# Moving VectorE's wait for its masked copy behind each level's operands, the queries' rotary work behind the fourth level, and the first branch unit ahead of the last gate part

## The reference

```python
hq, hf, hi, hz, aq, ak, av, az, ga, gb = split(rmsnorm(h) @ w_in)
f = lb + (1 - lb) * sigmoid(hf); kA = 1 - f
oA = hgrn2_chunked(hq, log(f), kA, hi)        # S_t = diag(f_t) S_{t-1} + k_t^T v_t
oB = softmax(q1 k1^T) v - lam * softmax(q2 k2^T) v   # q, k with rotary on the first quarter of dims
yA = (rmsnorm(oA) * silu(hz)) @ w_branch_a
yB = (rmsnorm(oB) * silu(az)) @ w_branch_b
h = h + (sigmoid(ga) * yA + sigmoid(gb) * yB) @ w_out
out = rmsnorm(h, final_g)
```

## Time and profile before

| | |
|---|---|
| median of 3 runs | 718.7 us (718.34 to 718.92) |
| profiled execution | 718.66 us, span 716.5 us |
| busy share of the span | PE 97%, DVE 76%, ACT 62%, POOL 23% |
| granted TensorE clock, share of full speed | 0.998 |
| first matmul of head 3 and of head 4 (L845) | 223.38 and 282.39 us |
| chain that ended last | PE 85%, DVE 8%, issue 4% |

### The profile page before, as it was taken

How to read it: one execution, slowest core, us unless ns; L and a number is a source line. 1 busy time by engine, 2 the same in 40 slices (tenths; PEclk the granted TensorE clock), 3 DMA queues, 4 the chain that set the end, 5 groups by cost and what they waited for, 6 DMA issues and landing times.

```text
span 716.5 us, 15635 instructions
## 1 busy us (share of the span) xinstructions
PE 693.7 (97%) x5121; PEld 650.2 (91%) x5121; DVE 542.2 (76%) x1233; ACT 446.6 (62%) x1004; POOL 167.9 (23%) x193
## 2 busy tenths in 40 slices
PE   3999999999999999999999999999999999999996
PEld 2998998999999999999999999999999988888885
DVE  5899869978978978997997897898677662735342
ACT  5553775885796596688588569658776661223232
POOL 2011332233333333233332333323411000000000
PEclk9999999999999999999999999999999999999999
DMA  8357667877867877786877787787777452235103
GB/s 328 126 116 174 147 147 170 174 195 171 179 149 185 191 163 163 165 202 157 176 164 181 175 180 162 165 180 189 165 203 212 143 177 88 98 108 206 59 1 118
DMA packets 51657, 115.58 MB, mean 161 GB/s; under 512 B 5762, under 2 KB 6164, under 8 KB 51620
## 3 DMA queue, kind: packets, MB, share of 16 engines
q0 software_dynamic: 22896, 42.48, 35.1%
q1 hardware_dynamic: 27972, 71.44, 29.3%
q10 hardware_dynamic: 752, 1.18, 0.5%
HBM read 70.51 MB, written 2.10 MB: 101 GB/s over the span
## 4 chain that ended last, share of the span: by engine, by line
PE 85%; DVE 8%; issue 4%; DMA 1%; ACT 1%; DVEq 0%; POOL 0%; SPq 0%; POOLq 0%; ACTq 0%
PE ps L681 23%; PE ps L682 22%; PE ps L683 22%; PE ps L938 3%; PE ps L863 3%; PE ps L966 2%; DVE aa L1884 2%; PE ps L845 1%; DVE w_lo L398 1%; PE ps L955 1%; PE ps L967 1%; PE ps L899 1%; PE ps L898 1%; PE ps L879 1%; PE ps L908 1%
## 5 line engine op out<-in xcount | busy, mean ns | idle before, releaser
L390 ACT ACTIVATE w_hi<-w_raw 128x512 fp32r<-128x512 f32 x216 | 131.9, 622 | 88.6 <-PE ps L683 37.3
L681 PE MATMUL ps<-t_hi,w_hi 128*128 128x256 f32 x576 | 170.2, 296 | 2.3 <-DVE vT_a L1776 1.7
L683 PE MATMUL ps<-t_hi,w_lo 128*128 128x256 f32 x576 | 162.6, 282 | 0.0
L682 PE MATMUL ps<-t_lo,w_hi 128*128 128x256 f32 x576 | 162.6, 282 | 0.0
L681 PE MATMUL ps<-uT_hi,w_hi 128*128 128x272 f32 (+3 forms) x536 | 162.1, 302 | 0.0
L682 PE MATMUL ps<-uT_lo,w_hi 128*128 128x272 f32 (+3 forms) x536 | 155.6, 290 | 0.0
L683 PE MATMUL ps<-uT_hi,w_lo 128*128 128x272 f32 (+3 forms) x536 | 155.3, 290 | 0.0
L617 POOL DMA_DIRECT2D w_lo<-w_raw x84 | 77.6, 924 | 190.2 <-ACT w_lo L392 179.7
L681 PEld LDWEIGHTS ps<-t_hi,w_hi 128*128 128x128 f32 x576 | 109.5, 190 | 7.6 <-issue 6.1
L682 PEld LDWEIGHTS ps<-t_lo,w_hi 128*128 128x128 f32 x576 | 109.8, 191 | 0.0
L683 PEld LDWEIGHTS ps<-t_hi,w_lo 128*128 128x128 f32 x576 | 109.6, 190 | 0.0
(11 more groups left out here) (254 smaller groups left out, 1468.7 us busy)
## 6 DMA issues: line engine op xcount, KB each, us to landing
w_raw<-in_w_in SPq DMA_DIRECT2D x44, 512.0 KB, 4.8
w_lo<-w_raw POOLq DMA_DIRECT2D x84, 256.0 KB, 4.3
w_raw<-in_w_in SPq DMA_DIRECT2D x72, 256.0 KB, 4.4
w_sum<-in_w_in SPq DMA_DIRECT2D x36, 256.0 KB, 3.1
w_raw<-w_raw POOLq DMA_DIRECT2D x36, 256.0 KB, 3.7
w_sum<-w_raw POOLq DMA_DIRECT2D x36, 256.0 KB, 4.5
w_raw<-in_w_branch_a SPq DMA_DIRECT2D x8, 512.0 KB, 3.3
w_raw<-in_w_branch_b SPq DMA_DIRECT2D x8, 512.0 KB, 3.3
```

The lines of the kernel that those rows point to most:

```text
L390: act.activation(part_at(w_hi, j), part_src(pr, j), ACT.Copy).then_inc(pair_hi[j], 1)
L681: pe.matmul(dst, w[0], rhs[0], start=start, stop=False, skip_group_check=True)
L682: pe.matmul(dst, w[0], rhs[1], start=False, stop=False, skip_group_check=True)
L683: return pe.matmul(dst, w[1], rhs[0], start=False, stop=stop, skip_group_check=True)
```

## The change

Four things. In `next_level`, VectorE's wait on `lvl_taken` goes from ahead of the multiplies to ahead of the short product. In `steady`, `rotated_lo(0)`, the queries' shuffle, products and sum go to later places, and `part_lo(p_1_, 1)`, `take_level(3)` and `sum_4` to others. On TensorE levels 4 and 8 come one slot earlier (12 to 11 and 15 to 14) and scores s0 and s1 one later (26 to 27); on ScalarE `rotated_hi(h, 1)` goes ahead of `tanh_z`. At the end of the gates, branch unit 0 goes ahead of the last pair's part 4, on ScalarE and VectorE its split goes ahead accordingly, and the counts of `w_used` follow.

```diff
-B0 = UNITS_END + PARTS * ALL_PAIRS + PART_ORDER.index(4) + 1
+B0 = UNITS_END + PARTS * ALL_PAIRS + 1
-HG_AT = dict(zip(HG_STEPS, (2, 7, 12, 15, 18, 22, 25, 28, 30, 33, 35, 52)))
-AT_AT = dict(zip(AT_STEPS, (26, 26, 28, 33, 33, 35, 35, 37, 37, 39, 42, 46, 48, 55)))
+HG_AT = dict(zip(HG_STEPS, (2, 7, 11, 14, 18, 22, 25, 28, 30, 33, 35, 52)))
+AT_AT = dict(zip(AT_STEPS, (27, 27, 28, 33, 33, 35, 35, 37, 37, 39, 42, 46, 48, 55)))
...
-                return PART_ORDER.index(4) if isinstance(pr.q, int) and (pr.q, j) == (ALL_PAIRS - 1, 4) else 0
+                return 0
...
-            for half in range(2):
-                part(gate_pair(GATES - 1), 4, half, False)
...
                 last.then_inc(w_used, 2)
+                if u == 0:
+                    for half in range(2):
+                        part(gate_pair(GATES - 1), 4, half, False)
...
                 save_p50(p_1_)
+                rotated_hi(h, 1)
                 tanh_z(h, 0)
-                rotated_hi(h, 1)
                 part_hi(act, p_2, 1)
...
-                    free = B0 if u == 3 else UNITS_END + PARTS * (ALL_PAIRS - 1) + min(2 * SLOT_OF[u] + 2, PARTS)
+                    free = B0 + 2 if u == 3 else UNITS_END + PARTS * (ALL_PAIRS - 1) + min(2 * SLOT_OF[u] + 2, PARTS)
...
+                if not more:
+                    branch_hi(0)
                 gate_rest(n + 1, before)
                 gate_11(n + 2, pr)
...
-                    for u in range(3):
+                    for u in (1, 2):
                         branch_hi(u)
...
                     if m > 1:
                         dve.wait_ge(lvl_ready, 7 * h + LEVELS.index(m))
-                        if taken != 0:
-                            dve.wait_ge(lvl_taken, 7 * h + LEVELS.index(m))
                     dve.wait_ge(hg_done, hg(h, f"l{m}"))
...
+                    if m > 1 and taken != 0:
+                        dve.wait_ge(lvl_taken, 7 * h + LEVELS.index(m))
                     mark(dve.tensor_tensor(t_of[2 * m], tk[:, :, 0], tk[:, :, 1], ALU.mult))
...
                     next_level(2, 0)
-                    part_lo(dve, p_1_, 0, 1)
+                    part_lo(dve, p_1_, 0)
                     take_level(1)
                     dve.wait_ge(lvl_taken, 7 * h + 1)
-                    rotated_lo(0)
+                    part_lo(dve, p_1_, 1)
                     take_level(2)
                     q_given()
                     next_level(4)
                     sum_2(dve, p_1_)
                     c_12(0)
-                    swap_pairs(qT[:, :])
+                    take_level(3)
                     c_22(0)
-                    take_level(3)
                     part_lo(dve, p_1_, 5)
                     next_level(8)
+                    swap_pairs(qT[:, :])
+                    sum_4(dve, p_1_)
                     turn_pairs(qT[:, :], META)
-                    sum_4(dve, p_1_)
                     take_level(4)
                     next_level(16)
+                    add_pairs(qT[:, :]).then_inc(rotated, 1)
                     part_lo(dve, p_1_, 6)
-                    add_pairs(qT[:, :]).then_inc(rotated, 1)
                     take_level(5)
                     next_level(32)
+                    rotated_lo(0)
                     part_lo(dve, p_2, 0)
...
+                if not more:
+                    branch_lo(0)
                 c12(pr, gates_at(n + 2)[0][:, HALF:])
...
-            for u in range(UNIT_SLOTS):
+            for u in range(1, UNIT_SLOTS):
                 branch_lo(u)
```

## The result

The changed kernel takes 708.3 us (median of 4 runs, 707.37 to 708.35), the one before 718.5 beside it: a ratio of 0.9855 [0.9838, 0.9872], 10.2 us less. The forecast was 8.6 less. So the kernel gained 1.6 more than forecast.

A forecast was written before the change was run, and what follows sets the result against it. TensorE's time was the bound, with VectorE's 18.34 us chain ending last in each head. Seven heads at 1.13 plus 0.69 in the tail gave 8.60 off 718.66: 710.1 us, with 708.3 to 714.0 to hold 8 in 10.

The forecast's parts named there:

- What bounds the kernel: Whole loop: TensorE's time bounds it, about 57.6 us of work a head, with VectorE's 18.34 us chain ending last.
- The moved wait: VectorE's multiplies behind the masked copies of levels 4, 16, 32, 64 start earlier, saving 1.18 us a head.
- The rotary work: Queries' rotary operations on VectorE only change places; two chained waits swap, adding 0.05 us, so the chain becomes 17.21.
- What TensorE finds: Level groups find operands ready; key transposes go from 248.72 to 247.59, so each head is 1.13 us shorter.
- The thinnest margin: TensorE's level-32 group: level 16's copy ends at 240.66, TensorE asks at about 240.93, a margin of 0.27 us.
- The likeliest case's own range: Total time if the forecast case holds: 708.5 (TensorE's 1.3 a head plus the tail) to 711.8 us.
- Head 1: First steady head in the loop: the same chain as the others and hence the same gain, 1.13 us.
- The tail: Last gate part: branch unit 0 fills TensorE's 0.89 us gap while it waits for VectorE's difference; gain 0.69 us.
- rival (d): In the tail, the branch unit is not ready and TensorE gains nothing there: 710.8 us, chance 0.05.
- Rival (a): VectorE starts the multiply no earlier because it empties itself between operations anyway; only the tail wins: 718.0 us, chance 0.06.
- Rival (b): In the heads, a thin margin or late DMA returns 2 to 5 us: 712 to 715 us, chance 0.14.
- Rival (c): The transfer behind `sum_4(p_1)` ends last; 6.1 us to landing removes the heads' gain, 7 us gives 723.6; chance 0.05.

The follow-up runs named there:

- shorter chain: Changed kernel with the low half of part 1 of the third pair moved from ahead of the last masked copy to behind it: 708.05 us, ratio 0.9845.
- old slots: Changed kernel with TensorE's earlier places restored (levels 4 and 8 one slot later, scores 0 and 1 one earlier): 710.54 us, ratio 0.9884.
- both: Changed kernel with part 1's low half behind the last masked copy and, before the loop, ScalarE's third-part high half ahead of the second norm: 707.87, 707.27, 707.98 us.

## Why the prediction was right and where it was wrong

**What bounds the kernel: right.** TensorE's time, with VectorE's chain ending last at the transposes. Taking the chain down took the heads down, and once the chain was short enough nothing more was to be had ("shorter chain"). Of the wait of 0.1 to 0.3 us that I had forecast at the transposes 0.04 is left.

**The moved wait: right in kind, too small in size. This is where the sum failed.** The failed step reads: "For the longer copy (0.73) I take its length less the 0.09 by which operations overlap here (0.71 long, next one 0.62 later: 232.08 to 232.70), so 0.64." It is 0.52, in the changed kernel and in the one with the wait alone. Level 4 therefore saves 0.41, not 0.29; levels 16, 32 and 64 save 0.29 to 0.30 as said. The chain is 0.24 shorter than my 17.21, and the head gained 0.24 more than my 1.13: 0.12 of it is this term, 0.09 the next one, and 0.03 is spread over several rows. I took the overlap from a plain operation, while the trace of before had the very thing in head 0, an independent operation behind a masked copy of this length, 0.55 from start to start. Its VectorE timeline:

```profile
50.32 0.74 DVE L1884 COPY_PREDICATED aa<-masks,ps 128x256 f32<-128x256 uint8 x1
...
50.87 0.84 DVE L1914 STREAM_SHUFFLE e<-qT 128x512 f32<-128x512 f32 x1
```

**The rotary work: nearly right.** The sum counted its places at +0.05. It missed that what now stands behind level 1's copy is a weight's low half (L398, 0.78 behind the copy) and no longer the keys' (L1930, 0.87), 0.09 less. With 0.12 and 0.09 the chain would have been 17.21 - 0.21 = 17.00; it is 16.97. Both stand behind a wait of the same kind as the moved ones, `dve.wait_ge(lvl_taken, 7 * h + 1)` directly behind `take_level(1)`, which the change left where it was. Why one of the two starts 0.09 sooner than the other behind the same copy and the same wait stays open.

**What TensorE finds: right to a few hundredths.** With 2.33 taken off, I had the groups of levels 8, 16 and 32 at 231.91, 235.26 and 238.60; they stand at 231.92, 235.28 and 238.63. The thinnest margin, 0.27 at level 32, is 0.50 (the copy into sq ends at 238.13), again those two hundred nanoseconds. Only the transposes are off, 245.02 for 245.26, since their time came from the chain. The bound I set, "TensorE alone would allow about 1.3", was 1.41 (59.02 - 57.61), the low end of my own 247.3 to 247.45, which allows 1.27 to 1.42. So the head gained 1.37 where I had 1.13, and seven heads 9.3 where I had 7.9: 1.4 of the 1.6 us missed. The likeliest case's own range was to end at 1.3 a head plus the tail, and there is a slip in it: 718.66 - 7 x 1.3 - 0.69 is 708.9 and not 708.5. With the 1.41 that TensorE allows it would have ended at 708.1. The moved places, which I had not priced by themselves, carry 0.49 of the 1.37 ("old slots").

**Head 1: the right number, with another reason.** 1.14 against 1.13. I had counted the same chain; in fact its VectorE starts 1.53 late behind a transfer (1.51 in the kernel before, so the wait isn't new), and shows other waits than the later heads, among them 0.21 at level 32:

```profile
122.82 0.71 PE L863 MATMUL ps<-qq,sq 128*128 128x128 f32 x4 [0.21 <-DVE sq L1861]
```

**The tail: right.** 0.69 said, 0.79 in the changed kernel and 0.74 alone. VectorE's low half of unit 0 was done at 565.95 (564.73 and 1.22 long), 1.5 us ahead of TensorE's start at 567.45, so rival (d) had no footing.

**Rival (a), that the wait costs nothing:** refuted by the two kernels that differ from their bases in this wait alone: 0.82 a head won by moving it, 1.27 lost (58.92 against 57.65) by putting it back. The Trainium skill's page "VectorE: DVE Perf Modes", section "The DRAIN you can't avoid", says that the next operation isn't issued until the pipe has emptied, and that chaining without semaphores saves nothing. The same section adds that a next operation that isn't held back starts earlier, which the prediction left out; so only its word on semaphores speaks against the change. Here the multiply starts 0.11 before the end of a 0.44 long copy and 0.21 before that of a 0.73 long one, and with the wait 0.19 to 0.20 behind it. On the semaphores the measurement decides: the wait cost 0.29 and 0.41 us each time.

**Rival (b), the thin margins:** not seen in the steady heads, where no level's group waits. Level 32's margin is the one I measured (0.50); where the wait was put back and the chain was 1.29 longer, it was gone, and TensorE stood there for 0.24. In head 1 it is gone too (the row above).

**Rival (c), the transfer behind the sum:** nearer than I said. I counted 5.04 us from issue to need and "about 1 us ahead". The need comes at 4.85 (230.19 to 235.04) and the transfer lands 4.7 us after its issue in this head, and 4.9 in the first steady head, where the shuffle at 118.81 is followed by the sum at 119.67, 0.86 in place of 0.63. GpSimd's timeline in the changed kernel, the issue at 230.19; and from its chain that ended last (start, us, what), the transfer of the first steady head:

```profile
230.19 0.86 POOL L617 DMA_DIRECT2D w_lo<-w_raw  x1 [2.90 <-ACT w_lo L392]
```

```profile
114.74 4.90 DMA w_lo<-w_raw
...
119.67 0.06 DVE w_raw L414
```

In the changed kernel's repeat the sum came 0.11 late in the first steady head and 0.18 in the sixth (57.85). The first steady head is where this margin is too thin: in six of the ten profiles with the sum in its new place it started 0.11 to 0.73 late there, the most in the third run of "both" (5.5 us to landing). I had named a wait for this transfer as a sign that the prediction is wrong; it left the other heads alone but for that one. So the mechanism of (c) is real, and in the profiles but that third one it delays the sum by less than half a microsecond an execution. The median of all such transfers, 4.1, was the wrong row for this one.

## What to carry to other kernels

In this kernel a wait for the masked copy directly ahead on the same engine had a price of its own, 0.29 us behind a 0.44 us copy and 0.41 behind a 0.73 us one, and it could stand behind work that doesn't need that result. Look for all such waits: the one behind `take_level(1)` still stands, 0.78 from start to start where 0.52 would do by level 4's row. That is an estimate of 0.26 us of chain and was not run; with TensorE at 57.61 us it would be worth at most 0.04 a head. Where two engines pace a loop in turn, as here, moving the wait and reordering the work paid together (1.37 a head) what they didn't pay apart (0.82 and 0.10), so neither is to be judged alone. Price an operation by a row with the same predecessor anywhere in the trace, and work out how far the other engine lets the gain go as carefully as the gain itself.

## What the runs showed of the hardware

The masked copy of 128x256 lasts 0.73 to 0.75 us for the first two levels and 0.42 to 0.45 for the later ones; an operation that doesn't wait for it starts 0.52 to 0.55 and 0.33 after it. So it may begin 0.21 ahead of the end of the one and 0.11 of the other: the overlap isn't a constant. The low half that does wait for the longer copy (level 1's) starts 0.78 or 0.87 after it, and the multiply that did 0.93. No row names the wait behind level 1's copy; it is found in the code.

A group of level matmuls whose operands come late costs some 0.1 us more than the standing itself: it is 0.71 long and not 0.61, and the next part starts 0.47 behind it and not 0.36. The idle gap isn't needed for that. In the kernel with the old slots a group that follows the matmul ahead of it by the usual 0.12 is 0.69 long, and the next part starts 0.45 behind it. What differs is the row of the weight load (PEld). It starts 0.12 ahead of the group where nothing is late, and 0.02 ahead or together with it where the group is long. From the timelines of the changed kernel, of the one with the old slots, and of the one before:

```profile
238.51 0.54 PEld L863 LDWEIGHTS ps<-qq,sq 128*128 128x128 f32 x4
238.63 0.61 PE L863 MATMUL ps<-qq,sq 128*128 128x128 f32 x4
```

```profile
238.43 0.52 PEld L863 LDWEIGHTS ps<-qq,sq 128*128 128x128 f32 x4
238.45 0.69 PE L863 MATMUL ps<-qq,sq 128*128 128x128 f32 x4
```

```profile
238.49 0.52 PEld L863 LDWEIGHTS ps<-qq,sq 128*128 128x128 f32 x4 [0.50 <-DVE sq L1861]
```

So in these rows the extra 0.1 goes with a weight load that no longer runs ahead of its matmul. That is my reading; no run varied it by itself. The granted clock was 1.00 in both windows of the head, before and after (0.998 over the span), so the clock isn't the cause.
